# Fox attention: the largest scores reach all partitions by two DMAs through a scratch row in place of eight TensorE transposes, and the maxima are taken ahead of the division

## The chip, the cores and the metric

The kernel runs on one core of one Trainium2 chip. The metric is the device time of one execution in microseconds (us). The times of the kernel before are the median of three runs.

TensorE (PE in the rows; PEld is its weight load) does the matrix products and writes only to PSUM, which has eight banks of 128 partitions x 512 float32. VectorE (DVE), ScalarE (ACT) and GpSimd (POOL) do elementwise work and reductions. SyncE (SP) issues the DMAs of this program. The engines run side by side and wait for each other on semaphores, each in the order of its own instructions.

## The reference

The reference is two blocks of a language model over 1024 tokens of width 1024, in float32: a block with latent attention and a sliding window, a block with forgetting attention ("Fox"), and a second model block with an mLSTM, a cross attention and sixteen experts. The change touches only the Fox attention:

```
def causal_block_attention(q, k, v, log_cum=None):
    ...
        s = jnp.einsum('bqhd,bkhd->bhqk', qi, k) * scale
        s = s + ci[..., :, None] - lc_t[..., None, :]
        s = jnp.where(mask, s, -jnp.inf)
        p = jax.nn.softmax(s, axis=-1)
        return jnp.einsum('bhqk,bkhd->bqhd', p.astype(v.dtype), v)
```

There are 16 heads of dimension 64. The softmax of a query needs the largest of its scores over all keys, subtracted before the exponential.

## The kernel before, in words

The Fox stage runs from about 660 us to 1240 us of the span. It has 16 steps u = 0 to 15. A step handles one pair of heads (p = u // 2) and one half of the queries (g = u % 2, 512 queries); inside it h = 0, 1 are the two heads. The scores are held transposed: keys lie on the partitions (128 keys to a block b), queries along the free axis. An even step has four blocks per head, of 512, 384, 256 and 128 queries (the causal cut); an odd step has eight, five of 512 and then 384, 256 and 128.

A step does this for each head:

- TensorE makes the scores in a ring of four banks; ScalarE or VectorE takes them to SBUF (`act_fox_scores`, and `empty` in `dve_fox_largest`), and VectorE keeps a running maximum over the blocks in MR (L2030). That maximum is still one value per partition and query.
- TensorE turns MR in four 128 x 128 transposes into bank 4 + h (`pe_fox_turn_largest`), and VectorE reduces it along the free axis to MX: one negated maximum per query, four columns of 128 queries for each head (L2120). The queries now lie on the partitions, where they are of no use for scores that have queries along the free axis.
- `pe_fox_spread_largest` (L1882) spreads them: four more transposes of one column of MX each, repeated 128 times, put in bank 4 + h a tile in which every partition holds all 512 values.
- `dve_fox_move` (L2056) adds that tile from PSUM to the scores in SBUF (L2062), ScalarE takes the exponential (L1971), GpSimd sums the exponentials over the blocks (L2160, the copy L2156), and one step later TensorE makes the weighted values and the sums (`pe_fox_values`, `pe_fox_sums`).
- `dve_fox_out` (L2065) divides the outputs of the step before: a reciprocal (L2070) and two products (L2078, L2081).

Between these, TensorE works off the projections of the next pair of heads as "quads": `pe_quad(n, j)`, seven products j = 0 to 6 for each n, four matrix products of 128 x 512 each (eight MATMUL rows of the trace, since each float32 product has two), put alternately in banks 6 and 7. VectorE empties them in `dve_quad` (L1781 is j = 2, L1784 j = 3, L1787 and L1788 j = 4, L1790 j = 5, L1793 j = 6), and a product two further on waits for its bank: j = 6 waits for both instructions of j = 4 (L1752), and j = 0 of the next quad waits for j = 5 (L1737).

The order in a step is written out by hand. TensorE: scores, the values and sums of u - 1, the four and four turns, quad j = 2 and 3, the spread, quad j = 4 to 6, and in an odd step j = 0 of the next quad. VectorE: maxima, the division of u - 1, the two reduces, quad j = 2 and 3, the moves of head 0, quad j = 4, the moves of head 1, quad j = 5 and 6. Step 15 has no quad; TensorE does three parts of the output projection there instead (`pe_fox_out_ahead`). SyncE loads the weights of the quads, each load behind the quad before it (`sp_fox`, L1670).

Of the kernel before, what the change touches and what calls it, by code (L numbers as in the profile page):

```python
# [98 lines left out]
def program(nc, x, positions, e_g_in, e_w_in, e_g_q_a, e_w_q_up, e_g_kv_a, e_w_kv_up, e_sinks, e_w_out,  # L99
# [5 lines left out]
    with ctx:  # L105
# [18 lines left out]
        x3 = nc.dram_tensor("x3_scratch", (S, D), F32).ap()  # L124
        x4 = nc.dram_tensor("x4_scratch", (S, D), F32).ap()
        x5 = nc.dram_tensor("x5_scratch", (S + 384, D), F32).ap()

# [1411 lines left out]
        NLK = tiled(XB[2][:, 0:128], 8)  # L1541
        ONEF = XB[2][:, 128:192]
        MX = XB[2][:, 192:200]
        bfc = stats(1)
        d_wf, d_bf = event("forget_weights_landed"), event("forget_bias_landed")
        wf_zero = event("gate_weights_zeroed")
        d_aug = [event(f"decay_rows_landed_{i}") for i in range(4)]
        ff_proj, ff_biased, ff_exp, decay_done = event("forget_projected"), event("forget_biased"), event("forget_exp"), event("decay_summed")
        lc_turned, lc_out = (e.again() for e in (q_proj, q_roped))
        ring_made, ring_a, ring_v = (e.again() for e in (s_done, ex_done, mx_done))  # L1550
        last_sums, tanh_done = p_turned.again(), pt_a.again()
        quad_made, quad_a, quad_v = lat_proj.again(7 * 15), lat_sq.again(15), lat_eps.again(7 * 15)
        left_made, right_made = lat_root.again(15), lat_normed.again(4)
        kmax_done, kmax_turned, m_known, m_spread = (e.again() for e in (sw_max, sw_turned, sw_added, ws_done))
        st_moved, st_exp, st_sum, st_pv, st_out = (e.again() for e in (pt_v, sw_exp, sw_out, pv_done, og_done))
        vt_turned, vt_a = q_turned.again(), qt_a.again()
        gates_done = sw_gr.again()
# [112 lines left out]
        def sp_fox():  # L1670
            fox_made(Y, ("k", 0, 1))
            load_fox(0, 1)
            for n in range(QUADS - 2):
                Y.wait_ge(quad_made, 7 * n + 7)
                load_fox(1 - n % 2, (n + 3) // 2)
            Y.wait_ge(quad_made, 7 * QUADS - 7)
            load_k(w_o2[1][:, 0:4, :], o_w_out[0][0:512, 512:1024], d_w[3])
            Y.wait_ge(quad_made, 7 * QUADS)
            load_k(w_o2[1][:, 4:8, :], o_w_out[0][512:1024, 512:1024], d_w[1])
            load_k(w_o2[0], o_w_out[0][:, 0:512], d_w[0])  # L1680
            for t in range(2):
                load_tile(x1, t, out2)
            Y.wait_ge(vt_turned, 16)
            load(GN_O, row(g_final), d_g)

# [170 lines left out]
            m.then_inc((ring_made if u < 15 else last_sums).sem, 1)  # L1858

        def pe_fox_turn_values(p):  # L1860
            P.wait_ge(st_moved, fox_chunks_before(2 * p + 1))
            P.wait_ge(quad_v, 14 * p + 6)
            for half in range(2):
                for j in range(4):
                    t = 4 * half + j
                    m = tr(bank(4 + half)[:, 128 * j:128 * j + 128], VT[:, 128 * t:128 * t + 128])
                m.then_inc(vt_turned.sem, 1)

        def pe_fox_turn_largest(u):

            for h in range(2):
                P.wait_ge(kmax_done, 2 * u + h + 1)
                if u:
                    P.wait_ge(st_moved, fox_chunks_before(u - 1, h) + len(fox_chunks(u - 1)))
                else:
                    P.wait_ge(lc_out, 1)
                P.wait_ge(vt_a, 2 * ((u + 1) // 2) - 1 + h)
                for j in range(4):
                    m = tr(bank(4 + h)[:, 128 * j:128 * j + 128], MR[h][:, 128 * j:128 * j + 128])
                m.then_inc(kmax_turned.sem, 1)  # L1880

        def pe_fox_spread_largest(u):  # L1882

            for h in range(2):
                P.wait_ge(m_known, 2 * u + h + 1)
                for j in range(4):
                    m = tr(bank(4 + h)[:, 128 * j:128 * j + 128], MX[:, 4 * h + j:4 * h + j + 1].to_broadcast([128, 128]))
                m.then_inc(m_spread.sem, 1)

        def pe_fox():  # L1890
            meet(P, out1_over)
            pe_shares(1, bank(7), WF, 1)
            pe_forget(0)
            pe_forget(1)
            for w, n in (("k", 0), ("q", 1), ("k", 1)):
                pe_fox_unit((w, 0, n))
            P.wait_ge(decay_done, 2)
            for b in range(8):
                m = pe.transpose(bank(5)[:, 16 * b:16 * b + 16], LC[0:16, 128 * b:128 * b + 128], ident[0:16, 0:16])
            m.then_inc(lc_turned.sem, 1)  # L1900
            for u in range(FOX_STEPS):
                blocks, quad = fox_blocks(u), u < QUADS
                for c in range(len(blocks) // 4):
                    pe_fox_scores(u, blocks[4 * c:4 * c + 4])
                    if quad and u == 0:
                        pe_quad(u, c)
                    elif quad and u % 2 == 0:
                        pe_quad(u, 1, c, 2)
                    elif quad and c < 3:
                        pe_quad(u, c // 2, c % 2, 2)  # L1910
                if u % 2:
                    pe_fox_turn_values(u // 2)
                    if quad:
                        pe_quad(u, 1, 1, 2)
                if u:
                    pe_fox_values(u - 1)
                    pe_fox_sums(u - 1, fox_free(("d", u - 1)))
                pe_fox_turn_largest(u)
                if quad:
                    pe_quad(u, 2)  # L1920
                    pe_quad(u, 3)
                else:
                    pe_fox_out_ahead(1, 1)
                pe_fox_spread_largest(u)
                if quad:
                    for j in range(4, 7):
                        pe_quad(u, j)
                    if u % 2:
                        pe_quad(u + 1, 0)
                else:  # L1930
                    pe_fox_out_ahead(0, 1)
                    pe_fox_out_ahead(0, 0)
            P.wait_ge(quad_v, 7 * QUADS)
            pe_fox_values(15)
            pe_fox_out_ahead(1, 0, range(0, 4))
            pe_fox_sums(15, bank(7))
            pe_fox_out_ahead(1, 0, range(4, NK))
# [118 lines left out]
        def dve_fox_move(u, h):  # L2056

            g = u % 2
            V.wait_ge(m_spread, 2 * u + h + 1)
            for b, n, lo in fox_chunks(u):  # L2060
                w = sx(g, h, b, lo, n)
                vec.tensor_tensor(w, w, tiled(bank(4 + h)[:, lo:512], 1).to_broadcast([128, n, 512 - lo]),  # L2062
                                  ADD).then_inc(st_moved.sem, 1)

        def dve_fox_out(u):  # L2065

# [16 lines left out]
        def dve_fox():  # L2083
# [23 lines left out]
            for u in range(FOX_STEPS):  # L2107
# [3 lines left out]
                if u % 2:  # L2111
                    if u < QUADS:
                        dve_quad(u, 1)
                    for n in range(2):
                        dve_fox_gate(u // 2, n)
                if u:
                    dve_fox_out(u - 1)
                for h in range(2):
                    V.wait_ge(kmax_turned, 2 * u + h + 1)
                    vec.tensor_reduce(MX[:, 4 * h:4 * h + 4], tiled(bank(4 + h), 4), AXX, MAX,  # L2120
                                      negate=True).then_inc(m_known.sem, 1)
                if u < QUADS:
                    dve_quad(u, 2)
                    dve_quad(u, 3)
# [1852 lines left out]
```

## Time and profile before

| | us |
|---|---|
| median of 3 runs | 2470.73 (2470.6 to 2472.54) |
| the profiled execution | 2472.73, its span 2471.4 |
| PE busy | 2355.8 (95%) |
| DVE busy | 1255.4 (51%) |
| ACT busy | 582.4 (24%) |
| POOL busy | 636.1 (26%) |
| chain that ended last | PE 86% |

The busy share is an average over stages. A row of the timeline gives the start, the length, the engine, the source line and how many instructions were merged in it; what stands in brackets is idle time before it. The difference between the execution's own time and its span, 1.3 us, lies outside the span and is untouched by the change.

### The profile page before, as it was taken

Reading aid. Unit: us, or ns where it says so; the run is one execution under the profiler, and the core shown is the slowest. Engines: PE = TensorE matmul, PEld = TensorE weight load, DVE = VectorE, ACT = ScalarE, POOL = GpSimd, SP = SyncE. Lnnn points to the kernel's source line nnn. Section 1 sums busy time; section 2 is a strip of 40 time slices with the busy share of each in tenths; the row PEclk is TensorE's granted clock in tenths of the full one; section 3 lists DMA queues with packets and bytes.
Section 4 is the critical chain, followed back from the end, with each engine's and each line's share of the span. In section 5 each row is a group of like instructions: output and inputs, shape, how many; then the busy total and the mean of one; then the engine's idle time right before and its main releaser. Section 6 shows DMA issues by size and latency. Waiting matters only on the chain.

```text
span 2471.4 us, 26003 instructions
## 1 busy us (share of the span) xinstructions
PE 2355.8 (95%) x9795; PEld 1374.4 (56%) x9795; DVE 1255.4 (51%) x2594; ACT 582.4 (24%) x1345; POOL 636.1 (26%) x528
## 2 busy tenths in 40 slices
PE   8999999999999999999999899999999999699993
PEld 5676657754444444444444577754464554387782
DVE  5444425543577777877744466665601336611214
ACT  3344433321122122222212111111100121011113
POOL 1000000044543354444261000006341035212213
PEclk9999999999999999999999999999999999799997
DMA  5000200212110111011245000003250213648987
GB/s 170 1 1 1 85 35 1 58 66 75 34 34 18 35 34 34 18 35 34 77 112 149 34 5 23 13 34 128 101 182 32 68 45 128 222 135 260 277 255 214
DMA packets 144627, 201.77 MB, mean 82 GB/s; under 512 B 16752, under 2 KB 101616, under 8 KB 144496
## 3 DMA queue, kind: packets, MB, share of 16 engines
q1 hardware_dynamic: 137584, 174.87, 21.4%
q0 software_dynamic: 6912, 25.17, 4.2%
q8 instruction: 80, 1.31, 0.2%
q14 instruction: 51, 0.42, 0.1%
HBM read 162.27 MB, written 37.75 MB: 81 GB/s over the span
## 4 chain that ended last, share of the span: by engine, by line
PE 86%; DVE 4%; POOL 3%; issue 2%; ACT 1%; DMA 1%; POOLq 0%; DVEq 0%; ACTq 0%
PE banks L170 80%; PE banks L173 6%; DMA arena<-x_scratch,slots 1%; POOL arena L1429 1%; POOL arena L1447 0%; DVE arena L3808 0%; DVE arena L3815 0%; DVE arena L895 0%; POOL arena L1424 0%; POOL arena L1430 0%; POOL arena L1432 0%; DMA x_scratch<-arena,places 0%; POOL arena L1458 0%; ACT arena L3140 0%; POOL arena L1460 0%
## 5 line engine op out<-in xcount | busy, mean ns | idle before, releaser
L170 PE MATMUL banks<-arena 128*128 128x512 f32 (+13 forms) x8147 | 2193.7, 457 | 35.0 <-ACT arena L2389 5.5
L170 PEld LDWEIGHTS banks<-arena 128*128 128x128 f32 (+4 forms) x8147 | 1200.4, 183 | 931.2 <-issue 834.6
L173 PE MATMUL banks<-arena 128*128 128x128 f32 (+2 forms) x1552 | 222.4, 280 | 42.2 <-DVE arena L447 10.4
L173 PEld LDWEIGHTS banks<-arena 128*128 128x128 f32 (+2 forms) x1552 | 178.8, 142 | 114.7 <-issue 66.7
L2160 POOL TENSOR_TENSOR arena<-arena 128x512 f32<-128x512 f32 (+3 forms) x160 | 154.4, 967 | 166.1 <-ACT arena L1971 146.5
L258 POOL TENSOR_TENSOR arena<-arena 128x1 f32<-128x1 f32 (+1 forms) x88 | 65.0, 740 | 500.3 <-DVE arena L2696 326.4
L1424 POOL TENSOR_TENSOR arena<-arena 128x512 f32<-128x512 f32 x4 | 9.3, 2321 | 572.7 <-PE banks L173 453.2
L1971 ACT ACTIVATE arena<-arena 128x512 f32<-128x512 f32 (+4 forms) x160 | 81.6, 576 | 315.9 <-DVE arena L2062 314.7
L2030 DVE TENSOR_TENSOR arena<-arena 128x512 f32<-128x512 f32 (+3 forms) x160 | 105.7, 719 | 28.3 <-ACT arena L1963 28.3
L3521 POOL DMA_INDIRECT x_scratch<-arena,places x24 | 37.9, 1577 | 204.3 <-DVE arena L3674 204.3
L2062 DVE TENSOR_TENSOR arena<-arena,banks 128x512 f32<-128x512 f32 (+4 forms) x160 | 89.5, 624 | 1.1 <-PE banks L173 1.1
L2014 DVE SCALAR_TENSOR_TENSOR arena<-banks,arena 128x512 f32<-128x512 f32 (+3 forms) x128 | 61.4, 540 | 35.4 <-PE banks L170 35.4
L895 DVE TENSOR_REDUCE arena<-banks 128x1 f32<-128x128 f32 (+7 forms) x64 | 48.1, 756 | 39.2 <-PE banks L170 38.7
L881 ACT ACTIVATE arena<-banks,arena 128x128 f32<-128x128 f32 (+7 forms) x64 | 47.3, 740 | 77.7 <-DVE arena L895 50.3
L2070 DVE RECIPROCAL arena<-banks 128x512 f32<-128x512 f32 x15 | 50.3, 3351 | 11.0 <-PE banks L170 11.0
L1103 DVE SCALAR_TENSOR_TENSOR arena<-arena,banks 128x256 f32<-128x256 f32 (+1 forms) x64 | 22.8, 398 | 57.6 <-PE banks L170 57.6
L1181 ACT ACTIVATE arena<-banks 128x512 f32<-128x512 f32 x32 | 19.0, 594 | 138.4 <-PE banks L173 138.4
L3663 DVE SCALAR_TENSOR_TENSOR arena<-arena,banks 128x384 f32<-128x384 f32 x16 | 8.9, 554 | 77.2 <-ACT arena L3639 77.2
L3674 DVE TENSOR_SCALAR arena<-banks,arena 128x512 f32<-128x512 f32 x24 | 18.0, 751 | 54.2 <-PE banks L170 54.2
L1070 ACT ACTIVATE arena<-arena 128x256 f32<-128x256 f32 (+1 forms) x64 | 31.1, 487 | 55.9 <-DVE arena L1112 55.9
L1207 DVE SCALAR_TENSOR_TENSOR arena<-arena 128x1024 f32<-128x1024 f32 x16 | 26.8, 1674 | 32.9 <-POOL arena L258 32.9
L1192 ACT ACTIVATE arena<-arena 128x1024 f32<-128x1024 f32 x16 | 16.9, 1057 | 110.4 <-DVE arena L1390 46.2
(349 smaller groups left out, 1734.0 us busy)
## 6 DMA issues: line engine op xcount, KB each, us to landing
x_scratch<-arena SPq DMA_DIRECT2D x40, 512.0 KB, 2.9
arena<-in_o_w_in_dram SPq DMA_DIRECT2D x32, 512.0 KB, 5.5
arena<-x_scratch SPq DMA_DIRECT2D x32, 512.0 KB, 5.3
arena<-in_w_gate_dram SPq DMA_DIRECT2D x16, 1024.0 KB, 15.1
arena<-in_w_up_dram SPq DMA_DIRECT2D x16, 1024.0 KB, 17.3
arena<-in_w_down_dram SPq DMA_DIRECT2D x16, 1024.0 KB, 19.3
arena<-in_x_dram SPq DMA_DIRECT2D x16, 512.0 KB, 4.5
arena<-in_w_in_dram SPq DMA_DIRECT2D x16, 512.0 KB, 7.1
```

The costliest lines, as they stand in the source:

```text
L170: return pe.matmul(o, a, b, start=start, stop=stop)
L173: return pe.transpose(o, a, ident)
L258: return pool.tensor_tensor(y, v, mhalf[:, 0:v.shape[1]], ALU.pow)
L881: act.activation(mla.weights(s, h)[:, 0:n], bank(2 * h, 2)[:, 0:n], ACT.Exp, bias=a8[:, h:h + 1], accum_out=a8[:, 2 + h:3 + h]).then_inc(e ...
L895: vec.tensor_reduce(a8[:, h:h + 1], bank(2 * h, 2)[:, 0:n], AXX, MAX, negate=True).then_inc(mx_done.sem, 1)
L1971: act.activation(w, w, ACT.Exp).then_inc(st_exp.sem, 1)
L2014: vec.scalar_tensor_tensor(sx(g, h, b, lo)[:, 0, :], fox_bank(key)[:, lo:512], NLK[:, b, 2 * p + h:2 * p + h + 1], MKT[:, 0:512 - lo], ADD ...
L2030: m = vec.tensor_tensor(mr, sx(g, h, 0, 0)[:, 0, :] if g and b == 1 else mr, s, MAX)
L2062: vec.tensor_tensor(w, w, tiled(bank(4 + h)[:, lo:512], 1).to_broadcast([128, n, 512 - lo]), ADD).then_inc(st_moved.sem, 1)
L2070: vec.reciprocal(RC, fox_bank(("d", u))).then_inc(ring_v.sem, 1)
L2160: m = pool.tensor_tensor(su, sx(g, h, 0, 0)[:, 0, :] if g and c == 1 else su, s, ADD)
L3521: pool.indirect_dma_start(out=x5, out_offset=bass.IndirectOffsetOnAxis(ap=PUT[:, c:c + 1].bitcast(U32), axis=0), in_=YS[i % 3], in_offset= ...
```

## The change

Eight transposes of the spread go from each step. In their place SyncE waits for MX, writes it to a row of a scratch tensor in DRAM, waits for that, and loads each head's 512 values back with a broadcast to all partitions, into the SBUF buffers MXB. The values land in the order (query in block, block), so the move reads them with a step of four words, and each block is now its own instruction. On VectorE the two reduces stand ahead of the division of the step before. Two waits of TensorE on the moves become waits on the reduces, since banks 4 and 5 are free once these are done.

```
+        MXB = [scr(58, 512), XB[2][:, 512:1024]]
+        d_largest, d_spread = d_aug[2], d_aug[0:2]
...
             for n in range(QUADS - 2):
+                sp_fox_largest(n)
                 Y.wait_ge(quad_made, 7 * n + 7)
                 load_fox(1 - n % 2, (n + 3) // 2)
+            sp_fox_largest(QUADS - 2)
...
+        def sp_fox_largest(u):
+            Y.wait_ge(m_known, 2 * u + 2)
+            sync.dma_start(largest_rows[u].rearrange("(h p j) -> p h j", h=2, j=4),
+                           tiled(MX, 2), allow_slow_non_contiguous=True).then_inc(d_largest.sem, 16)
+            Y.wait_ge(d_largest, 16 * u + 16)
+            for h in range(2):
+                load(MXB[h], row(largest_rows[u][512 * h:512 * h + 512]), d_spread[h])
...
         def pe_fox_turn_values(p):
-            P.wait_ge(st_moved, fox_chunks_before(2 * p + 1))
+            P.wait_ge(m_known, 4 * p + 2)
...
-                    P.wait_ge(st_moved, fox_chunks_before(u - 1, h) + len(fox_chunks(u - 1)))
+                    P.wait_ge(m_known, 2 * u - 1 + h)
...
-        def pe_fox_spread_largest(u):
-            for h in range(2):
-                P.wait_ge(m_known, 2 * u + h + 1)
-                for j in range(4):
-                    m = tr(bank(4 + h)[:, 128 * j:128 * j + 128], MX[:, 4 * h + j:4 * h + j + 1].to_broadcast([128, 128]))
-                m.then_inc(m_spread.sem, 1)
...
         def dve_fox_move(u, h):
-            V.wait_ge(m_spread, 2 * u + h + 1)
+            V.wait_ge(d_spread[h], 16 * u + 16)
             for b, n, lo in fox_chunks(u):
                 w = sx(g, h, b, lo, n)
-                vec.tensor_tensor(w, w, tiled(bank(4 + h)[:, lo:512], 1).to_broadcast([128, n, 512 - lo]),
-                                  ADD).then_inc(st_moved.sem, 1)
+                largest = MXB[h].rearrange("p (q j) -> p j q", j=4)[:, lo // 128:4, :]
+                for c in range(n):
+                    o = w[:, c, :].rearrange("p (j q) -> p j q", q=128)
+                    m = vec.tensor_tensor(o, o, largest, ADD)
+                m.then_inc(st_moved.sem, 1)
...
-                if u:
-                    dve_fox_out(u - 1)
                 for h in range(2):
                     V.wait_ge(kmax_turned, 2 * u + h + 1)
                     vec.tensor_reduce(MX[:, 4 * h:4 * h + 4], ...)
+                if u:
+                    dve_fox_out(u - 1)
```

VectorE in step 5 (an odd one), before, from the second gate product on. Semaphores are used again under their first names: window_turned is the turned maxima, window_scores the spread, latents_projected the quad products, latents_variance their emptying.

```order
L1826 SCALAR_TENSOR_TENSOR arena<-arena 128x512 [waits turned_weights_by_act] x2
L2070 RECIPROCAL arena<-banks 128x512 [waits scores]
L2078 TENSOR_TENSOR arena<-arena 128x512 [waits window_gates_by_sums,row_max]
L2081 TENSOR_TENSOR arena<-arena,banks 128x512 [waits vector_step,weighted_values]
L2120 TENSOR_REDUCE arena<-banks 128x4 [waits window_turned] x2
L1781 SCALAR_TENSOR_TENSOR arena<-banks,arena 128x512 [waits latents_projected]
L1784 SCALAR_TENSOR_TENSOR arena<-banks,arena 128x512 [waits latents_variance,latents_projected]
L2062 TENSOR_TENSOR arena<-arena,banks 128x1024 [waits window_scores]
L2062 TENSOR_TENSOR arena<-arena,banks 128x1024
L2062 TENSOR_TENSOR arena<-arena,banks 128x512
L2062 TENSOR_TENSOR arena<-arena,banks 128x384
L2062 TENSOR_TENSOR arena<-arena,banks 128x256
```

The same place in the changed kernel; the lines are its own (L2131 is the reduce, L2083 the reciprocal, L2075 the move), and decay_rows_landed_0 is the broadcast load of head 0.

```order
L2131 TENSOR_REDUCE arena<-banks 128x4 [waits window_turned] x2
L2083 RECIPROCAL arena<-banks 128x512 [waits scores]
L2091 TENSOR_TENSOR arena<-arena 128x512 [waits window_gates_by_sums,row_max]
L2094 TENSOR_TENSOR arena<-arena,banks 128x512 [waits vector_step,weighted_values]
L1800 SCALAR_TENSOR_TENSOR arena<-banks,arena 128x512 [waits latents_projected]
L1803 SCALAR_TENSOR_TENSOR arena<-banks,arena 128x512 [waits latents_variance,latents_projected]
L2075 TENSOR_TENSOR arena<-arena 128x512 [waits decay_rows_landed_0]
L2075 TENSOR_TENSOR arena<-arena 128x512 x4
L2075 TENSOR_TENSOR arena<-arena 128x384
L2075 TENSOR_TENSOR arena<-arena 128x256
L2075 TENSOR_TENSOR arena<-arena 128x128
L1806 SCALAR_TENSOR_TENSOR arena<-arena,banks 128x512 [waits latents_variance,latents_projected]
```

The reduces moved ahead of the reciprocal and its two products. Six moves with one input from the arena (SBUF) and one from the banks (PSUM) became eight with both inputs from the arena; the emptying of quad j = 4 stands behind them in both. SyncE has, new in each step between the loads of weights:

```order
L1699 DMA largest_scratch<-arena 128x2x4 [waits window_masked]
L251 DMA arena<-largest_scratch 128x512 [waits decay_rows_landed_2]
L251 DMA arena<-largest_scratch 128x512
L254 DMA arena<-in_o_w_in_dram 128x8x128 [waits latents_projected]
L254 DMA arena<-in_o_w_in_dram 128x8x128
```

The store waits for both reduces (window_masked is MX), the two loads for the store, and the weights follow once the step's quad is done.

## Rows read from the trace of the kernel before

**Rows 1.** The page's chain that ended last, by engine.

```profile
PE 86%; DVE 4%; POOL 3%; issue 2%; ACT 1%; DMA 1%; POOLq 0%; DVEq 0%; ACTq 0%
```

**Rows 2.** Busy by stretch, the Fox stage: PE, PEld, DVE, ACT, POOL, PEclk, DMA.

```profile
660.00:1240.00 580.00, 576.43 (x2016) 260.54 (x2018) 433.51 (x666) 148.48 (x274) 242.91 (x228) 1.00 0.13 36
```

**Rows 3.** Timeline of step 5, an odd one, PE, DVE and POOL.

```profile
855.93 1.09 PE L173 MATMUL banks<-arena 128*128 128x128 f32 x8
857.06 3.35 DVE L2070 RECIPROCAL arena<-banks 128x512 f32<-128x512 f32 x1
861.84 1.28 DVE L2120 TENSOR_REDUCE arena<-banks 128x4 f32<-128x512 f32 x2
863.73 1.04 PE L173 MATMUL banks<-arena 128*128 128x128 f32 x8
863.93 0.69 DVE L1784 SCALAR_TENSOR_TENSOR arena<-banks,arena 128x512 f32<-128x512 f32 x1 [0.21 <-PE banks L170]
864.54 3.93 DVE L2062 TENSOR_TENSOR arena<-arena,banks 128x1024 f32<-128x1024 f32 x6
864.60 26.88 PE L170 MATMUL banks<-arena 128*128 128x512 f32 x92
866.92 16.08 POOL L2160 TENSOR_TENSOR arena<-arena 128x512 f32<-128x512 f32 x14 [17.25 <-ACT arena L1971]
868.39 0.68 DVE L1787 SCALAR_TENSOR_TENSOR arena<-arena,banks 128x512 f32<-128x512 f32 x1
869.59 3.93 DVE L2062 TENSOR_TENSOR arena<-arena,banks 128x1024 f32<-128x1024 f32 x6
```

**Rows 4.** Timeline of step 6, an even one, PE and DVE.

```profile
891.41 1.10 PE L173 MATMUL banks<-arena 128*128 128x128 f32 x8
896.32 1.28 DVE L2120 TENSOR_REDUCE arena<-banks 128x4 f32<-128x512 f32 x2
900.02 1.67 DVE L2062 TENSOR_TENSOR arena<-arena,banks 128x512 f32<-128x512 f32 x4
903.73 0.69 DVE L1787 SCALAR_TENSOR_TENSOR arena<-arena,banks 128x512 f32<-128x512 f32 x1 [2.03 <-PE banks L170]
```

**Rows 5.** Groups by line and shape, DVE, 680 to 1240 us.

```profile
L2062 DVE TENSOR_TENSOR arena<-arena,banks 128x1024 f32<-128x1024 f32 x32 | 37.5, 1211 | 1.1 <-PE banks L173 1.1
L2062 DVE TENSOR_TENSOR arena<-arena,banks 128x512 f32<-128x512 f32 x32 | 21.7, 678 | 0.0
```

**Rows 6.** Timeline, steps 5 and 6: running maxima on DVE, weight sums on POOL.

```profile
852.04 3.29 DVE L2030 TENSOR_TENSOR arena<-arena 128x512 f32<-128x512 f32 x8
...
884.50 5.32 DVE L2030 TENSOR_TENSOR arena<-arena 128x384 f32<-128x384 f32 x6
...
886.14 1.58 POOL L1805 TENSOR_TENSOR arena<-arena 128x512 f32<-128x512 f32 x1
...
887.80 1.34 POOL L1807 TENSOR_TENSOR arena<-arena 128x512 f32<-128x512 f32 x1
```

**Rows 7.** DMA issues: KB each, median us to landing.

```profile
x_scratch<-arena SPq DMA_DIRECT2D x40, 512.0 KB, 2.9
...
arena<-in_o_g_in_dram SPq DMA_DIRECT2D x1, 512.0 KB, 4.2
...
arena<-in_pool_w_dram SPq DMA_DIRECT2D x1, 256.0 KB, 2.7
...
arena<-in_w_in_dram SPq DMA_DIRECT2D x2, 16.0 KB, 3.6
```

**Rows 8.** Timeline of step 15, DVE and PE.

```profile
1216.33 3.35 DVE L2070 RECIPROCAL arena<-banks 128x512 f32<-128x512 f32 x1
...
1222.86 1.04 PE L173 MATMUL banks<-arena 128*128 128x128 f32 x8
```

**Rows 9.** Busy by stretch around a PE pause in a later stage.

```profile
1360.30:1365.50 5.20, 0.00 (x0) 0.00 (x0) 4.94 (x10) 0.30 (x3) 0.00 (x0) 1.00 0.00 0
1365.50:1368.90 3.40, 3.13 (x7) 2.52 (x8) 3.29 (x4) 0.53 (x4) 0.00 (x0) 0.50 0.00 0
```

More of the change, by code:

```diff
@@ L126, in program @@
         x5 = nc.dram_tensor("x5_scratch", (S + 384, D), F32).ap()
+        largest_rows = nc.dram_tensor("largest_scratch", (16, 1024), F32).ap()
         top = [0]
@@ L1547, in program @@
         d_aug = [event(f"decay_rows_landed_{i}") for i in range(4)]
+        d_largest, d_spread = d_aug[2], d_aug[0:2]
+        d_largest.block(16 * 16)
+        for d in d_spread:
+            d.block(16 * 16)
         ff_proj, ff_biased, ff_exp, decay_done = event("forget_projected"), event("forget_biased"), event("forget_exp"), event("decay_summed")
@@ L1553, in program @@
         left_made, right_made = lat_root.again(15), lat_normed.again(4)
-        kmax_done, kmax_turned, m_known, m_spread = (e.again() for e in (sw_max, sw_turned, sw_added, ws_done))
+        kmax_done, kmax_turned, m_known = (e.again() for e in (sw_max, sw_turned, sw_added))
         st_moved, st_exp, st_sum, st_pv, st_out = (e.again() for e in (pt_v, sw_exp, sw_out, pv_done, og_done))
@@ L1673, in sp_fox @@
             for n in range(QUADS - 2):
+                sp_fox_largest(n)
                 Y.wait_ge(quad_made, 7 * n + 7)
                 load_fox(1 - n % 2, (n + 3) // 2)
+            sp_fox_largest(QUADS - 2)
             Y.wait_ge(quad_made, 7 * QUADS - 7)
             load_k(w_o2[1][:, 0:4, :], o_w_out[0][0:512, 512:1024], d_w[3])
+            sp_fox_largest(QUADS - 1)
             Y.wait_ge(quad_made, 7 * QUADS)
@@ L1682, in sp_fox @@
                 load_tile(x1, t, out2)
+            sp_fox_largest(15)
             Y.wait_ge(vt_turned, 16)
             load(GN_O, row(g_final), d_g)
+        def sp_fox_largest(u):
[5 more added lines that the diff above has]
+                load(MXB[h], row(largest_rows[u][512 * h:512 * h + 512]), d_spread[h])
         FS = [scr(46 + 2 * n, 512) for n in range(2)]
@@ L1923, in pe_fox @@
                     pe_fox_out_ahead(1, 1)
-                pe_fox_spread_largest(u)
                 if quad:
```

## The prediction

> **What bounds the kernel now.** I read the chain of waits first: TensorE carries 86% of it [rows 1]. Then the busy time of the Fox stage alone: 576.4 of 580 us on TensorE, at full clock [rows 2]. So in this stage every TensorE instruction taken away is time gained, and every pause of TensorE is time lost, with 3.6 us of idle time there to lose it in. Then the timeline of an odd and an even step [rows 3, 4], to see what TensorE will wait for once the spread is a DMA. VectorE is close behind it in an odd step: the moves of head 0 start at 864.54, those of head 1 at 869.59, and each has a quad's emptying behind it for which TensorE waits two products later.
>
> **What goes.** The eight transposes of the spread: in step 5 the products behind them start at 864.60, the transposes at 863.73, so 0.87 us a step [rows 3]. Over 16 steps, 13.9 us. The LDWEIGHTS go with them and lie beside other work.
>
> **The reduces ahead of the division.** The turned maxima are ready at 857.02 (855.93 + 1.09), and VectorE comes free of the gate products at 857.06; the two reduces take 1.28 us, so MX is known at 858.34 and not at 863.12 [rows 3]. The division only trades places with them, so quad j = 2 is emptied at the same time as before, 863.7, which is when TensorE now wants its bank. Nothing gained or lost. In an even step the reduces start when the first head is turned, about 892.05, and end at 893.4 [rows 4]; the division had started 0.5 us earlier, which TensorE may feel by up to 0.3 us. I take 0.
>
> **The DMA round trip.** One store of 4 KB in 256 pieces of 16 bytes, then two broadcast loads of 256 KB. The trace has no such store. Nearest are a load of 16 KB in short pieces, 3.6 us, and stores of 512 KB, 2.9 us; for the loads, a broadcast of 512 KB at 4.2 us (the same bytes as both here) and a load of 256 KB at 2.7 us [rows 7]. I take 3.6 + 4.2 = 7.8 us, from the rows nearest in shape; the low end is 2.7 + 2.7 = 5.4, the high end, the short pieces costing three times a plain load and the broadcast as it is, 8.1 + 4.2, about 12. The weights on the same queue were issued a step earlier or come later, so nothing stands ahead. The moves of an odd step then begin at 858.34 + 7.8 = 866.1 and not at 864.54; those of an even step at 901.2 and not at 900.02.
>
> The Trainium skill's page SBUF — State Buffer, section The DMA setup-cost knee, puts a DMA at 2 us and the bytes at 436 GB/s. By it the round trip would be about 5.2 us, close to my low end, and the sum 21 us lower (2.6 us in each of eight steps).
>
> **The moves themselves.** Before, a move reads SBUF and PSUM and keeps its pace beside GpSimd's sums: 3.93 us for six, with POOL at work from 866.92 on [rows 3]; 678 ns for 512 columns, 1211 ns for 1024, so 1.04 ns a column [rows 5]. Now both inputs are in SBUF, as in the running maxima L2030. Those show the price: eight of them with POOL idle took 3.29 us. Take two of 512 away (about 0.6 us each, start to start) and the other six are worth 2.1; the same six beside POOL's tensor_tensor took 5.32 us [rows 6]. The two engines alternate there, one instruction for one: a POOL instruction of 512 columns is 1.27 to 1.34 us and becomes 1.58 when it has to let one of 256 or 384 columns pass. So a move behind a 512-wide POOL sum costs 1.35 us plus its own columns.
>
> Step 5, with T = 866.1 the start of the moves:
> - Head 0: the sum can start once the first two blocks are moved and exponentiated, T + 2.4 as before (866.92 - 864.54). By then five moves are under way: 2.9 us. The moves of 384, 256 and 128 columns each stand behind a 512-wide sum: 3 x 1.35 + 0.8 = 4.85. Head 0 ends at T + 7.75 = 873.9 (before 868.5).
> - The two instructions of quad j = 4 read PSUM and run free, 1.3 us: 875.15. TensorE reaches j = 6 at 863.73 + 16 x 0.43 = 870.6 (eight MATMUL of 0.43 us a product) and stands 4.6 us, to 875.2; j = 6 ends at 878.6.
> - Head 1: eight moves, 3.5 us of reading, behind what is left of head 0's sums (about 2.1 us) and four 512-wide sums of head 1 (4 x 1.3 = 5.2): 10.8 us, to 885.95. Quad j = 5 is emptied at 886.65.
> - TensorE wants the bank of j = 5 for the next quad's j = 0 at 878.6 and gets it at 886.75: 8.1 us. It ends at 890.2; before it ended at 864.60 + 32 x 0.43 = 878.36. An odd step is 11.8 us longer, the removed transposes already in it.
>
> The exponentials and POOL's sums of the step (until about 889) are wanted only later in step 6, several us behind the restart, so nothing is added there.
>
> **The clock.** After a pause of 5.2 us TensorE worked at a granted clock of 0.50, its lower level (1.2 GHz), for 3.4 us and had 1.00 before it paused [rows 9]. I expect the same behind each 8 us pause: 1.7 us. The low clock after the first pause is hidden, since j = 6 has 8 us to spare. Odd step: 13.5 us. The bounds of this term are 0 and 3.4 us.
>
> **Even steps.** Four moves take 1.67 us and the first head's are over before POOL's sums are dense; VectorE waits 2.03 us for quad j = 4 afterwards [rows 4]. The 1.2 us later start fits into that pause, and the second head's moves meet one or two short sums. Each even step keeps its 0.87 us.
>
> **Step 15.** No quad, but TensorE stands before the values of step 15. The reduces start when the reciprocal did, 1216.4, MX is known at 1217.7 [rows 8], the moves start at 1225.5 and both heads need 7.75 + 10.8, the last exponential 0.3: 1244.35. TensorE was there at 1223.73 + 13.76 = 1237.5. So +6.9, and 1.7 for the clock: +8.6.
>
> **Sum.** Seven odd steps with quads (u = 1 to 13) x 13.5 = 94.5; step 15 +8.6; eight even steps x 0.87 = -7.0. In all +96.1 us. On the profiled execution, 2472.73, that is 2568.8; the median of the runs is 2.0 us lower, so 2567.
>
> **Rivals.**
>
> *The strided read costs too.* The move reads MXB with a step of four words. No row shows such a read at length. If it halves the pace, 3.5 us are added to the reads of each half-step of eight moves, and POOL waits as long: +7.0 us in each of eight odd steps, 2567 + 56 = 2623. For it: nothing in the trace excludes it. Against: nothing shows it. The same page, in the section Door 1: The DMA port swizzle, says that accesses within a 16-byte line are at full rate and each new line costs extra; with a step of four words every element is in a new line. No run here shows it so far.
>
> *A slow round trip.* At 12 us instead of 7.8 the odd steps lose 4.2 us more each (34 us in eight), and in even steps the moves start at 905.4, quad j = 4 is emptied at 908.4, where TensorE wants it at 905.9: 2.5 us in eight steps. 2567 + 54 = 2621.
>
> *The other side: the two engines do not get in each other's way.* The place is the moves of odd steps. If they run at 3.9 to 4.1 us beside POOL, as the PSUM form does, and the round trip is 5.4 us, then VectorE is at head 0 from 864.5 to 868.6, j = 4 is empty at 869.9 (wanted at 870.6), head 1 ends at 874.0 and j = 5 at 874.7 (wanted at 874.05). The step keeps 0.2 us; seven of them 1.4, eight even ones 7.0, step 15 0.9: -9.3, a time of 2461. It decides whether a move beside a sum takes under about 0.8 us on average. With 7.8 us of round trip and no hindrance an odd step loses 1.5 us, and all is +2.6, 2473, no change. Against both: rows 6 show instructions of the very same form slowed to 5.32 us for 2.1.
>
> *The change does not do what it says* has no room here: the listing shows the transposes gone and the DMAs in place.
>
> **How the numbers follow.** Forecast as above 0.60; strided read dear 0.15; slow round trip 0.10; hindrance absent with a short trip 0.08 (faster); hindrance absent with the long trip 0.07 (no change). What a measurement of this kernel can tell from no change is about 0.2%, 5 us. Faster 0.08, within 0.07, slower 0.85. The range: the forecast's own low end is a trip of 5.4 us (-2.4 in eight steps, 19 us) without the clock's 13.6 us, 2534. The high end takes in the two slower rivals, 2625. Outside it lie the two cases of 0.15.
>
> **What would show it.** In the profile after: L2075, the moves, about 1.1 us on average where L2062 of 512 columns had 0.68; TensorE idle twice in each odd step, 4 to 5 us ended by the emptying of j = 4 (L1807) and about 8 us ended by that of j = 5 (L1809); about 48 us from the reduces of step 5 to those of step 6, where it was 896.32 - 861.84 = 34.5 [rows 3, 4]; the granted clock below 1.00 in slices of this stage; the store landing in 3 to 4 us and the loads in about 4. It is wrong if moves of 512 columns stay near 0.7 us, or if TensorE's pauses are ended by something else, the sums or the exponentials.

## The result and the profile after

The changed kernel takes 2535.15 us, median of four runs (2532.29 to 2547.46), against 2471.11 for the kernel before on the same chip: ratio 1.0266, 95% interval 1.024 to 1.0292, 64 us slower. The profiled execution took 2537.29 us with a span of 2536.0, so the two traces differ by 64.6 us. The sign was forecast; of the size, +96, two thirds came.

The page of the changed kernel: busy time, share of the span and instructions of each engine, and the chain by engine, which answers to [rows 1].

```profile
PE 2365.2 (93%) x9667; PEld 1369.0 (54%) x9667; DVE 1343.0 (53%) x2626; ACT 592.3 (23%) x1345; POOL 729.1 (29%) x528
...
PE 78%; DVE 10%; POOL 4%; issue 3%; DMA 2%; ACT 1%; POOLq 0%; DVEq 0%; ACTq 0%
```

VectorE now carries 10% of the chain where it carried 4%. At which instruction TensorE waits for it is in the waits of TensorE over the Fox stage, 660 to 1325 us: waiting line, releasing line, us in all, times, the longest one.

```profile
PE banks L171 <- DVE arena L1809: 29.3, 7, 7.8
PE banks L171 <- DVE arena L1807: 14.6, 7, 4.8
PE banks L171 <- POOL arena L2173: 9.0, 2, 6.9
```

L1807 is the emptying of quad j = 4, L1809 that of j = 5, each seven times, once in each odd step: the two places that the prediction named. L2173 is GpSimd's sum of the weights.

The timeline of step 5 after (start us, us, instruction, idle time before it and what ended it), which answers to [rows 3]:

```profile
866.91 1.09 PE L174 MATMUL banks<-arena 128*128 128x128 f32 x8
...
868.05 1.27 DVE L2131 TENSOR_REDUCE arena<-banks 128x4 f32<-128x512 f32 x2
869.25 3.34 DVE L2083 RECIPROCAL arena<-banks 128x512 f32<-128x512 f32 x1
...
875.52 6.73 DVE L2075 TENSOR_TENSOR arena<-arena 128x512 f32<-128x512 f32 x8
...
878.77 25.90 POOL L2173 TENSOR_TENSOR arena<-arena 128x512 f32<-128x512 f32 x14 [18.11 <-ACT arena L1981]
...
883.35 6.69 DVE L2075 TENSOR_TENSOR arena<-arena 128x512 f32<-128x512 f32 x8
883.50 3.70 PE L171 MATMUL banks<-arena 128*128 128x512 f32 x8 [1.59 <-DVE arena L1807]
...
889.90 0.74 DVE L1809 SCALAR_TENSOR_TENSOR arena<-banks,arena 128x512 f32<-128x512 f32 x1
...
890.78 11.68 PE L171 MATMUL banks<-arena 128*128 128x512 f32 x32 [3.59 <-DVE arena L1809]
...
909.36 1.09 PE L174 MATMUL banks<-arena 128*128 128x128 f32 x8
```

The first row and the last are TensorE's turn of the maxima, of step 5 and of step 6. Read the rest from VectorE. The reduces end at 869.32, and the moves start 6.2 us later, right behind the division, its two products and two emptyings. That is 8.61 us behind the start of TensorE's turn, as it was before (855.93 to 864.54, [rows 3]): the DMAs delay nothing here. Both heads take 6.7 us each, where they took 3.93. POOL is the one that suffers: its 14 sums take 25.90 us where they took 16.08. TensorE stands 1.6 and 3.6 us. Step 7 looks otherwise:

```profile
954.19 9.92 DVE L2075 TENSOR_TENSOR arena<-arena 128x512 f32<-128x512 f32 x8
...
965.23 12.54 DVE L2075 TENSOR_TENSOR arena<-arena 128x512 f32<-128x512 f32 x8
...
965.37 5.40 PE L171 MATMUL banks<-arena 128*128 128x512 f32 x8 [4.79 <-DVE arena L1807]
...
978.52 6.86 PE L171 MATMUL banks<-arena 128*128 128x512 f32 x12 [7.76 <-DVE arena L1809]
```

Here the moves took 9.92 and 12.54 us and TensorE stood 4.8 and 7.8 us. How long GpSimd's sums took shows the difference: the summary of line L2173 (instructions, duration in ns of the single ones as min/median/max), first of step 5, then of step 7, then of step 15.

```profile
L2173 POOL TENSOR_TENSOR arena<-arena x14: 457/1262/7651, 878.8 to 904.1; 128x512 f32<-128x512 f32 x8, 128x384 f32<-128x384 f32 x2, 128x256 f32<-128x256 f32 x2, 128x128 f32<-128x128 f32 x2
...
L2173 POOL TENSOR_TENSOR arena<-arena x13: 726/1519/3018, 957.4 to 978.8; 128x512 f32<-128x512 f32 x8, 128x384 f32<-128x384 f32 x2, 128x256 f32<-128x256 f32 x2, 128x128 f32<-128x128 f32 x1
...
L2173 POOL TENSOR_TENSOR arena<-arena x14: 454/1262/13457, 1278.3 to 1307.9; 128x512 f32<-128x512 f32 x8, 128x384 f32<-128x384 f32 x2, 128x256 f32<-128x256 f32 x2, 128x128 f32<-128x128 f32 x2
```

In step 5 the median sum takes 1.26 us and the longest 7.65: it is held out while the moves of head 1 run through, from 883.53 to 891.18, and ends 1.14 us behind the last of them. The sum before it lasts 4.62 us beside head 0 and also ends 1.14 us behind the last move. In step 7 the longest is 3.02 us: the engines alternate. In step 15 one sum lasts 13.46 us, from 1278.3 on: across the moves, which end at 1288.4, and the addition over SBUF right behind them (L1360), to 1.13 us behind its end. Even steps are no such clear case: the four moves of their head 1 take 3.5 to 4.2 us, where they take 2.7 with GpSimd kept away (experiment 2), so sums do get turns there. The clock behind the 3.59 us pause of step 5, with the columns of [rows 9]:

```profile
887.20:890.60 3.40, 0.00 (x0) 0.00 (x0) 3.40 (x7) 2.77 (x5) 3.40 (x1) 1.00 0.62 165
890.70:894.00 3.30, 3.21 (x4) 1.50 (x5) 0.53 (x1) 0.00 (x0) 3.01 (x3) 0.50 0.55 137
```

**Where the 64.6 us are.** From TensorE's turn of the maxima of one step to that of the next (L173 before, L174 now) an odd step took 35.48 us before; now six of seven take 42.4 to 42.5, and step 7 takes 51.65. Even steps went from 37.12 to 36.23. So 6 x 7.0 + 16.2 = 58.1 in odd steps, -7.1 in the eight even ones, and the stage begins 0.4 us earlier. The 7.0 us of an odd step are 1.6 + 3.6 us of pauses, 1.7 for the clock and 0.87 less for the transposes, 6.0, and 1.0 of small rests. (From reduces to reduces the kernels can't be compared step by step, because the change moves the reduces ahead of the division, and step 0 has no division.) TensorE's turn of the maxima of step 15 starts at 1265.73 and started at 1215.06: 50.7 us of the 64.6. The other 13.9 are step 15 and what follows it; its timeline:

```profile
1265.73 1.09 PE L174 MATMUL banks<-arena 128*128 128x128 f32 x8
...
1278.32 30.06 POOL L2173 TENSOR_TENSOR arena<-arena 128x512 f32<-128x512 f32 x14 [25.53 <-ACT arena L1981]
...
1308.43 14.22 PE L171 MATMUL banks<-arena 128*64 128x512 f32 x26 [6.90 <-POOL arena L2173]
```

There TensorE stands 0.97, 2.08 and 6.90 us, the last two for sums that come late behind the one that was held out; the granted clock is 0.50 from 1303.66 to 1313.90.

The DMAs of a step, two loads and a store, KB each and median us to landing:

```profile
arena<-largest_scratch SPq DMA_DIRECT2D x32, 256.0 KB, 3.9
...
largest_scratch<-arena SPq DMA_DIRECT2D x16, 4.0 KB, 2.0
```

### The profile page after: what moved, and what is told of

Read it like the earlier page. It is cut to its first block, busy times and chain, and to the rows that moved or that the text cites. A ratio compares the mean times of both kernels' runs of the same rounds, so it can differ in the third digit from the quotient of the medians.

```text
span 2536.0 us, 25827 instructions
## 1 busy us (share of the span) xinstructions
PE 2365.2 (93%) x9667; PEld 1369.0 (54%) x9667; DVE 1343.0 (53%) x2626; ACT 592.3 (23%) x1345; POOL 729.1 (29%) x528
## 4 chain that ended last, share of the span: by engine, by line
PE 78%; DVE 10%; POOL 4%; issue 3%; DMA 2%; ACT 1%; POOLq 0%; DVEq 0%; ACTq 0%
PE banks L171 72%; PE banks L174 5%; DVE arena L2075 4%; POOL arena L2173 1%; DMA arena<-x_scratch,slots 1%; DVE arena L2024 1%; POOL arena L1430 1%; POOL arena L1448 1%; DVE arena L3821 0%; DVE arena L3828 0%; DVE arena L896 0%; POOL arena L1425 0%; POOL arena L1431 0%; DVE arena L2035 0%; POOL arena L1433 0%
## 5 line engine op out<-in xcount | busy, mean ns | idle before, releaser
L2173 POOL TENSOR_TENSOR arena<-arena 128x512 f32<-128x512 f32 (+3 forms) x160 | 238.6, 1494 | 171.9 <-ACT arena L1981 152.3
L174 PE MATMUL banks<-arena 128*128 128x128 f32 (+1 forms) x1424 | 205.7, 280 | 41.9 <-DVE arena L448 10.3
L174 PEld LDWEIGHTS banks<-arena 128*128 128x128 f32 (+1 forms) x1424 | 164.0, 142 | 105.6 <-issue 55.2
L1981 ACT ACTIVATE arena<-arena 128x512 f32<-128x512 f32 (+4 forms) x160 | 90.8, 585 | 367.2 <-DVE arena L2075 364.0
L2075 DVE TENSOR_TENSOR arena<-arena 128x512 f32<-128x512 f32 x192 | 170.0, 969 | 2.0 <-DMA arena<-largest_scratch 2.0
L2083 DVE RECIPROCAL arena<-banks 128x512 f32<-128x512 f32 x15 | 50.1, 3343 | 0.0
L2169 POOL COPY arena<-arena 128x512 f32<-128x512 f32 x16 | 20.7, 1293 | 97.4 <-ACT arena L1981 97.4
```

What stands on the lines that cost most here:

```text
L174: return pe.transpose(o, a, ident)
L1981: act.activation(w, w, ACT.Exp).then_inc(st_exp.sem, 1)
L2075: m = vec.tensor_tensor(o, o, largest, ADD)
L2083: vec.reciprocal(RC, fox_bank(("d", u))).then_inc(ring_v.sem, 1)
L2173: m = pool.tensor_tensor(su, sx(g, h, 0, 0)[:, 0, :] if g and c == 1 else su, s, ADD)
```

## The experiments

Two theories stood at first. **A:** the moves are long because they read MXB with a step of four words, and VectorE, once at it, keeps GpSimd out. **B:** they are long because the two engines take turns on SBUF, as forecast. Times of before in the two groups of runs: 2472.31 and 2472.14 us.

**1. Contiguous read (e1).** The scratch row is written so that MXB is read without a step.

```diff
-largest_rows[u].rearrange("(h p j) -> p h j", h=2, j=4)
+largest_rows[u].rearrange("(h j p) -> p h j", h=2, j=4)
...
-largest = MXB[h].rearrange("p (q j) -> p j q", j=4)[:, lo // 128:4, :]
+largest = MXB[h].rearrange("p (j q) -> p j q", q=128)[:, lo // 128:4, :]
```

> The changed kernel with the scratch row written block by block (1024 pieces of 4 bytes instead of 256 of 16), so that a move reads the broadcast values one after another and not with a step of four words; both inputs stay in SBUF. Theory A (the step of four words doubles the time of a move, VectorE keeps the shared read path and GpSimd is the one that waits): the eight moves of a head in an odd step take 3.9 to 4.2 us instead of 6.7, the store lands about 1 us later, TensorE's two pauses in an odd step shrink from 1.6 and 3.6 us to about 0.2 and 1.7, time about 2475 us (2465 to 2490). Theory B (my prediction's: a move alternates with GpSimd's sums, one for one, whatever its step): the moves of head 1 still take 10 us or more, and the time is 2540 us or more.

Measured: 2651.3 us (2649.76 to 2651.74), ratio 1.0725 [1.0707, 1.0743]. The store among its DMAs, and then an even step's first head and an odd step in its timeline:

```profile
largest_scratch<-arena SPq DMA_DIRECT2D x16, 4.0 KB, 10.1
```

```profile
877.24 1.70 DVE L2075 TENSOR_TENSOR arena<-arena 128x512 f32<-128x512 f32 x4 [6.77 <-DMA arena<-largest_scratch]
...
920.02 7.32 DVE L2075 TENSOR_TENSOR arena<-arena 128x512 f32<-128x512 f32 x8 [7.77 <-DMA arena<-largest_scratch]
928.45 9.99 DVE L2075 TENSOR_TENSOR arena<-arena 128x512 f32<-128x512 f32 x8
...
928.59 5.71 PE L171 MATMUL banks<-arena 128*128 128x512 f32 x8 [10.05 <-DVE arena L1807]
939.20 6.00 PE L171 MATMUL banks<-arena 128*128 128x512 f32 x10 [4.90 <-DVE arena L1809]
```

Three things. The store is cut into 1024 pieces of 4 bytes instead of 256 of 16, and lands after 10.1 us instead of 2.0, where about 1 us more was expected: VectorE waits 113.4 us in all for the loads behind it. Together with the alternation in the odd steps this makes the kernel slow, so its time decides nothing between A and B; the moves do. With POOL idle until their last 0.3 us, four moves take 1.70 us, as the ones that read PSUM did (1.67, [rows 4]). And beside POOL, eight moves take 7.32 and 9.99 us: the contiguous moves do alternate with the sums, close to the forecast's 7.75 and 10.8. So each theory is right about one form of the move, and A's "VectorE keeps GpSimd out" isn't a property of VectorE whatever it runs.

**2. GpSimd kept away (e2).** The sums of a step wait until all its exponentials are through.

```diff
+G.wait_ge(st_exp, fox_chunks_before(u + 1))
 for h in range(2):
     for i, (b, n, lo) in enumerate(fox_chunks(u)):
-        G.wait_ge(st_exp, fox_chunks_before(u, h) + i + 1)
```

> The changed kernel with GpSimd waiting, before the first sum of a step, for all exponentials of the step, so that no sum runs beside a move. Theory A (the strided read alone sets the length of a move): the moves keep 6.7 us for eight, TensorE's pauses in odd steps stay 1.6 and 3.6 us, only step 7's extra 9 us goes, and the sums of step 15 come later: 2520 to 2535 us. Theory B (GpSimd's sums are what slows the moves): the moves fall to about 4 us for eight and the time below 2500 us.

Measured: 2523.82 us (2521.16 to 2528.43), ratio 1.0207 [1.019, 1.0224]. The timeline of its step 5 with the first head of step 6, and then the group of its 512-column moves (instructions, busy us, mean ns of one, idle time before them):

```profile
876.42 6.76 DVE L2075 TENSOR_TENSOR arena<-arena 128x512 f32<-128x512 f32 x8
...
884.26 6.70 DVE L2075 TENSOR_TENSOR arena<-arena 128x512 f32<-128x512 f32 x8
884.44 3.70 PE L171 MATMUL banks<-arena 128*128 128x512 f32 x8 [1.65 <-DVE arena L1807]
891.70 3.55 PE L171 MATMUL banks<-arena 128*128 128x512 f32 x4 [3.57 <-DVE arena L1809]
...
918.49 2.69 DVE L2075 TENSOR_TENSOR arena<-arena 128x512 f32<-128x512 f32 x4
```

```profile
L2075 DVE TENSOR_TENSOR arena<-arena 128x512 f32<-128x512 f32 x96 | 99.2, 1100 | 1.6 <-DMA arena<-largest_scratch 1.6
```

With no sum anywhere near, eight moves still take 6.7 us and TensorE's pauses stay at 1.6 and 3.6. Four take 2.69 where e1's contiguous ones took 1.70. So in six of the seven odd steps the pauses come from the strided read alone: (512 x 5 + 384 + 256 + 128) columns in 6.7 us are 2.0 ns a column, against 1.2 before (3.93 us) [rows 3]. Between the two profiled executions e2 is 8.9 us faster than the change, and that is step 7, which is a step like the others here.

**3. The division first again (e3).** Only the order of the reduces is undone.

```diff
+if u:
+    dve_fox_out(u - 1)
 for h in range(2):
...
-if u:
-    dve_fox_out(u - 1)
```

> The changed kernel with the order of VectorE as before: the division of the step before stands ahead of the two reduces. The store then leaves 4.8 us later in an odd step and about 3.8 us later in an even one. Both theories: an odd step loses 4 to 5 us more, an even one about 2 us (it has 2 us of slack for quad j = 4), so 2580 to 2600 us. If the order is worth nothing, 2535 us.

Measured: 2586.55 us (2570.87 to 2594.54), ratio 1.0475 [1.0455, 1.0494]. TensorE's waits in it:

```profile
PE banks L171 <- DVE arena L1807: 58.0, 14, 10.2
PE banks L171 <- DVE arena L1809: 10.2, 7, 2.6
```

With the DMA spread the early reduces are worth 51 us by the medians and 33.6 between the two profiled executions (2570.87 is the fastest of e3's four runs). Not all of it is the round trip. From reduces to reduces its even steps 2 to 12 take 38.4 to 39.3 us, at least 2 more than the 36.2 of the changed kernel; four of its odd steps take 43.2 to 43.4, about 1 us more than the usual 42.5 there and not the 4 to 5 that were expected; and in the other three the moves of head 0 took 10.9 us, so there the strided ones alternated too, and these steps take about 49. The expected stretch was met, but in part by this alternation.

**4. The early reduces alone (e4).** In the kernel before, with TensorE's spread.

```diff
-if u:
-    dve_fox_out(u - 1)
 for h in range(2):
...
+if u:
+    dve_fox_out(u - 1)
```

> The kernel before with the reduces ahead of the division and nothing else: the spread stays on TensorE. All theories: the transposes stand behind quad j = 3 on TensorE, so the moves start where they did; 2471 us, within 3 us. If the early reduces were a gain by themselves, 2460 us or less.

Measured: 2472.93 us (2470.64 to 2477.53), ratio 1.0006 [0.9996, 1.0015]. The prediction's "the division only trades places with them" holds.

**5. The interleaved values put in order on the way to PSUM (e5).** ScalarE copies MXB into banks 4 and 5, and the moves are those of before. ScalarE takes the step of four words, and the moves have one input in PSUM again. TensorE's two waits are again on the moves, since these read banks 4 and 5.

```diff
+C.wait_ge(d_spread[h], 16 * u + 16)
+act.activation(bank(4 + h).rearrange("p (j q) -> p j q", q=128),
+               MXB[h].rearrange("p (q j) -> p j q", j=4), ACT.Copy).then_inc(m_spread.sem, 1)
...
```

> The changed kernel with one more step: ScalarE copies each head's 512 broadcast values from SBUF into bank 4 + h, in the order in which they are used, and the moves are again the six of before with one input in PSUM. The DMA round trip and the early reduces stay. If the moves' SBUF input is the whole loss (its step of four words, and the read path shared with GpSimd), the moves take 3.93 us again and start about 7 us behind the reduces, TensorE does not wait for quad j = 4, waits at most 0.9 us for j = 5 in odd steps, and the time is 2458 to 2467 us. If the round trip by itself costs, 2480 us or more.

Measured: 2468.58 us (2463.94 to 2471.18), ratio 0.9979 [0.9969, 0.9988]. The timeline of its step 5, and then TensorE's waits:

```profile
861.96 3.95 DVE L2077 TENSOR_TENSOR arena<-arena,banks 128x1024 f32<-128x1024 f32 x6 [0.55 <-ACT banks L2006]
864.35 16.09 POOL L2175 TENSOR_TENSOR arena<-arena 128x512 f32<-128x512 f32 x14 [17.89 <-ACT arena L1981]
...
867.01 3.94 DVE L2077 TENSOR_TENSOR arena<-arena,banks 128x1024 f32<-128x1024 f32 x6
```

```profile
PE banks L171 <- DVE arena L1809: 3.4, 7, 0.8
```

The moves are back at 3.94 us, the sums at 16.09 and the wait for j = 4 is gone. The same DMAs, landing after 1.9 and 3.8 us, are now in a kernel a little faster than the one before. So the store and the loads cost TensorE little, some 0.5 us in an odd step; the form of the move was the loss. The time is 1.6 us above the expected stretch (2458 to 2467): most of the 13.9 us doesn't show at the end.

**6. The same, and j = 5 emptied earlier (e6).** In odd steps quad j = 5 is emptied behind the first move of head 1, one of 1024 columns.

```diff
-dve_fox_move(u, 1)
-dve_quad(u, 5)
+dve_fox_move(u, 1, 0, 1)
+dve_quad(u, 5)
+dve_fox_move(u, 1, 1)
 dve_quad(u, 6)
...
```

> As e5_values_to_psum, and in odd steps VectorE empties quad j = 5 behind the first move of head 1, and j = 6 behind its last. If only the wait for j = 5 is left, it goes and all 13.9 us of the removed transposes show: 2456 to 2461 us. If something else is next (the sums, the scores' ring), it stays at e5's time or above.

Measured: 2464.24 us (2461.59 to 2467.0), ratio 0.9965 [0.9951, 0.9978]: faster than both kernels. Its timeline in step 5, and the last row from the stage behind Fox:

```profile
849.74 25.40 PE L171 MATMUL banks<-arena 128*128 128x512 f32 x68
...
857.04 2.13 ACT L2006 ACTIVATE banks<-arena 128x512 f32<-128x512 f32 x2 [12.35 <-DMA arena<-largest_scratch]
858.17 3.94 DVE L2077 TENSOR_TENSOR arena<-arena,banks 128x1024 f32<-128x1024 f32 x6 [0.66 <-ACT banks L2006]
...
1254.07 1.94 PE L174 MATMUL banks<-arena 128*128 128x128 f32 x8 [2.45 <-issue]
```

TensorE runs through step 5 without a pause. Its turn of step 15 starts at 1200.44, 14.6 us earlier than before. Of these, 3.0 are not the edit's: the turn of step 0 already starts 1.3 us earlier, and step 0 is 1.7 us shorter than the other even steps explain; e4, whose edit gains nothing, also has a lead of 2.8 us over the kernel before in step 0. The other 11.6 stand against 15 x 0.87 = 13.0 us of transposes. Only 8.5 us are left at the end of the span. The same instructions of VectorE start 14.7 us earlier at 1238 us, 12.5 at 1291, 11.0 at 1417, 9.8 at 1802 and 8.4 at 2359 (times of before): the lead is lost in small parts through the later stages. One of them is the last row: that pause was 1.82 us before and the eight transposes behind it took 1.06 us, now it is 2.45 and they take 1.94. The others were not followed up, and why 3 us are missing from the expected 2461 stays open.

**7. A gap between the moves (e7).** In each head the moves signal in six groups (two of two and four of one in an odd step). Each group now waits until the one ahead of it on the same engine has signalled that it is done; nothing else changes.

```diff
-for b, n, lo in fox_chunks(u):
+for i, (b, n, lo) in enumerate(fox_chunks(u)):
+    V.wait_ge(st_moved, fox_chunks_before(u, h) + i)
```

> The changed kernel with VectorE waiting, ahead of each block's move, for the one before it to be complete. If GpSimd is kept out because the moves follow each other without a gap, the waits let it in and every odd step with quads looks like step 7 (head 0 about 10 us, head 1 about 12.5, 51 us from reduces to reduces): 2580 to 2600 us. If the gap has nothing to do with it, the moves take about 7.2 us for eight and the time stays below 2550 us.

Measured: 2598.44 us (2597.34 to 2601.75), ratio 1.0512 [1.0496, 1.0528]. An odd step in its timeline, and then TensorE's waits:

```profile
893.29 11.13 DVE L2076 TENSOR_TENSOR arena<-arena 128x512 f32<-128x512 f32 x8
...
896.54 10.90 POOL L2174 TENSOR_TENSOR arena<-arena 128x512 f32<-128x512 f32 x7 [18.11 <-ACT arena L1981]
...
905.53 11.82 DVE L2076 TENSOR_TENSOR arena<-arena 128x512 f32<-128x512 f32 x8
```

```profile
PE banks L171 <- DVE arena L1809: 48.1, 7, 6.9
PE banks L171 <- DVE arena L1807: 41.8, 7, 6.1
```

Now every odd step is like step 7: 52 us from reduces to reduces, and GpSimd's seven sums of a head pass in 10.9 us beside the moves. Strided moves with a gap between them alternate in all eight odd steps; without one, in the changed kernel, they do in one of eight.

**8. The emptyings among the strided moves (e8).** As in e6, in the changed kernel: j = 4 behind half the blocks of head 0, j = 5 behind head 0, j = 6 among those of head 1.

```diff
+if u < QUADS and u % 2:
+    dve_fox_move(u, 0, 0, 2)
     dve_quad(u, 4)
+    dve_fox_move(u, 0, 2)
     dve_quad(u, 5)
+    dve_fox_move(u, 1, 0, 2)
     dve_quad(u, 6)
+    dve_fox_move(u, 1, 2)
...
```

> The changed kernel with strided moves as they are, and in odd steps with quad j = 4 emptied behind the first four moves of head 0, j = 5 behind head 0, j = 6 behind the first four moves of head 1. TensorE's two pauses behind j = 4 and j = 5 go. If they are the whole loss, 2460 us. If GpSimd, kept out until the moves end at about 22 us behind the reduces, is next, TensorE waits about 6 us for the sums of the odd step in the step after it: 2500 to 2525 us.

Measured: 2517.25 us (2514.03 to 2521.68), ratio 1.0184 [1.0168, 1.02]. The timeline of VectorE in step 5, and then TensorE's waits:

```profile
871.19 4.09 DVE L2075 TENSOR_TENSOR arena<-arena 128x512 f32<-128x512 f32 x4
...
879.59 7.50 DVE L2075 TENSOR_TENSOR arena<-arena 128x512 f32<-128x512 f32 x4
```

```profile
PE banks L171 <- DVE arena L1812: 23.4, 7, 3.4
PE banks L171 <- POOL arena L2182: 8.1, 2, 6.0
```

The two pauses are gone and a third, for j = 6, takes the place: four moves of 512 columns that took 4.09 us in head 0 take 7.50 in head 1, since GpSimd gets its turns there. The emptyings, which read PSUM, let it in: the first sum meets the moves at 874.44 and ends at 876.42, 1.14 us behind the fourth move, while VectorE empties j = 4. The first move of head 1 then meets a running sum and takes 1.59 us, and the two alternate from there. No run varies this alone. The time fell into the expected stretch, but by this wait and not by the late sums that I had named. A better order doesn't mend a slow move.

## Why the prediction was right in sign and half as much again too high

- **What goes** (13.9 us of transposes): right. Each even step of the changed kernel is 0.89 us shorter, against 0.87; e6 has 11.6 of 13.0 us at step 15.
- **The reduces ahead of the division** ("nothing gained or lost"): right by itself (e4), and with the DMA it is what hides the trip (e3, though not all of its 51 us).
- **The DMA round trip**, 7.8 us: too long. The store took 2.0 us, the loads 3.9; with 6.2 us from reduces to moves it hides behind the division, and VectorE waited for a load once in the whole stage, 2.0 us in step 15. The estimate from the Trainium skill's page SBUF — State Buffer, section The DMA setup-cost knee, about 5.2 us for both, is nearer: the two landings add up to 5.9.
- **The moves themselves: this is the step that failed.** It took the read at the normal pace and laid GpSimd's sums one for one between the moves: 7.75 and 10.8 us. The runs show 6.7 and 6.7 in six of seven odd steps, made up otherwise: the strided read costs 2.0 ns a column with GpSimd away altogether (e2), and GpSimd gets almost no turn there. So TensorE's two pauses are 1.6 and 3.6 us where the forecast had 4.6 and 8.1, and an odd step is 7.0 us longer where it had 13.5. The alternation with its sizes exists, 7.32 and 9.99 us in e1's contiguous form, 9.92 and 12.54 in step 7, 11.1 and 11.8 in e7.
- **The strided read costs too**, a rival at 0.15, had its mechanism right, and nearly its size (3.5 us forecast for eight moves; 6.7 against 3.93 is 2.8), and the rule beside it, from the section Door 1: The DMA port swizzle of the same page of the Trainium skill (each new 16-byte line costs extra), agrees with the runs in direction: 1.0 us more for four moves of 1280 columns. But I added its 56 us on top of the alternation; in the runs it mostly came instead of it. Two costs of one instruction were treated as a sum where the one had changed the terms of the other.
- **The two pauses:** right in place and in what ends them, 1.6 and 3.6 us instead of 4.6 and 8.1; in step 7, where the alternation happened, 4.8 and 7.8.
- **The clock:** right, 0.50 for 3.3 us behind the second pause as in [rows 9], though the pause was only 3.6 us long.
- **Even steps:** right: no pause for the emptying of a quad, and -7.1 against -7.0 us.
- **Step 15 and after:** forecast +8.6, measured +13.9, by another way: not VectorE's moves but the sum held out behind them, and the clock.
- In sum: odd steps 58.1 against 94.5, even ones -7.1 against -7.0, step 15 and after 13.9 against 8.6, and -0.4 ahead of the stage: 64.6 against 96.1.

That 2535.15 lies inside the stated range, 2534 to 2625, is luck. It is 1.15 us above the low end, and two of the four runs, 2532.29 and 2533.01, lie below it. The low end was worked out as a short trip without the clock's cost. The trip was short, but the clock's cost came, and the moves were shorter than the low end, too, took them to be. What lifted the time back over the low end was the alternation of step 7, 9.2 us more than the other odd steps, and the late sums of step 15, which the prediction did not have. With GpSimd kept away from the moves (e2) it is 2523.82.

**Open:** what decides whether a sum gets its turn between moves that follow each other without a wait. Contiguous moves alternate (e1). Strided ones do in head 1 of every even step of the changed kernel, where a sum is already running when the first move starts (that move takes 1.2 to 1.6 us and not 1.1), in step 7, and in three steps of e3. In the other odd steps they don't, though the first sum starts 3.23 us behind the first move in step 7 and 3.25 in step 5. That the spread of the changed kernel's runs, 2532 to 2547, comes from how many steps fall the one way or the other is likely and only argued: one such step is worth 9 us.

## What to carry to other kernels

When a small vector is spread through DRAM, the layout has to suit three users at once: the store (pieces of 16 bytes or of 4), the load, and the engine that reads it many times; a step of four words on the reader, over 3328 columns of a head in odd steps, cost more than the eight transposes it replaced (e2, with no sum beside a move, is still 51.5 us slower than the kernel before). Look at what memory the operands of a busy instruction move to, not only at the instruction removed: one input moved from PSUM to SBUF made VectorE and GpSimd rivals, and 14 sums that took 16.1 us took 25.9. An idle engine, ScalarE here, can put the values in order and into PSUM, which took away both costs and left a kernel 3.6 us faster than before, 7.9 with j = 5 emptied earlier, of the 13.9 that had been removed.

## What the runs showed of the hardware that was not expected

- 4 KB written to DRAM landed in 2.0 us as 256 pieces of 16 bytes, and in 10.1 us as 1024 pieces of 4 bytes.
- A VectorE tensor_tensor over SBUF with one operand at a step of four words took 2.0 ns a column: 2.69 us for four of 1280 columns in all (e2), against 1.70 us read in order (e1), with GpSimd idle or nearly so; ScalarE copied 2 x 512 such values to PSUM in 2.13 us.
- VectorE and GpSimd do not always share SBUF by turns: a GpSimd sum that takes 1.26 us at the median lasted 7.65 us, and 13.46 us in step 15, beside moves in close order, and ended 1.13 to 1.14 us behind the last of them or the addition behind it; once a semaphore wait stood between the moves, the sums got their turns in every odd step (e7).
